# A triangular solve in pairs of heads: the second head set six rounds behind the first

## The chip, the cores and the metric

The kernel runs on one core of a Trainium2 chip. The metric is the device time of one execution in microseconds (us), the median of several runs. The engines are named as in the profile: PE (TensorE, with PEld for its weight loads), DVE (VectorE), ACT (ScalarE), POOL (GpSimd) and SP (SyncE).

## The reference

The kernel computes three layers on 512 tokens of width 1024 (two mixer layers and a third with routed experts). The change touches one step of the first layer, inside the RWKV-7 part, which has 8 heads of width 64. The core of it:

```python
A_ab = pair(a_dec, b_inv, strict)      # strictly lower triangular
A_ak = pair(a_dec, k_inv, strict)
A_rb = pair(r_dec, b_inv, incl)
A_rk = pair(r_dec, k_inv, incl)
rhs = jnp.concatenate([a_dec, jnp.einsum('bhnls,bhnsv->bhnlv', A_ak, v)], axis=-1)
sol = lax.linalg.triangular_solve(jnp.eye(L, dtype=F32) - A_ab, rhs,
                                  left_side=True, lower=True, unit_diagonal=True)
z_state, z_local = sol[..., :N], sol[..., N:]
y_local = jnp.einsum('bhnls,bhnsv->bhnlv', A_rk, v)
```

So for each head a unit lower triangular matrix is inverted by products, and the inverse is applied to two right-hand sides. The scan over chunks that follows uses z_state, z_local, A_rb and y_local.

## The kernel before

The kernel is a list of stages. In each stage every engine has a queue written out by hand, and at the end of each stage PE, ACT and DVE meet at a barrier (`meet`, L2717): each one adds to `stage_done` and waits until all three have done so. The solve, `rwkv_solve`, is one such stage; `rwkv_prepare` is before it and `rwkv_scan` after it.

The solve works on chunks of 64 tokens; a 128x128 tile holds two chunks on its diagonal, and the 512 tokens are four tiles (`TT`). All products of one kind for a head are four f32 matmuls (`mm`), which fill one PSUM bank of 128x512; the trace shows each of the four as two matmul records, so one `mm` is 8 records. A transpose is one record.

The eight heads are four pairs: `a` counts pairs (0 to 3), `q` the two heads of a pair (0 and 1). Head `q` has four of the eight banks (`4 * q` on) and seven buffers of its own (`buf[q]`: M, D, ET, AK, X, M2, D2), which all pairs use again. The heads of a pair also sit on different halves of the partitions (`r`) in the inputs and in two outputs.

A head is solved in 11 rounds, `g` = 1 to 11. In each round PE multiplies (L1516 to L1546), and then DVE, ACT or both move the results from the banks to SBUF, where the head's next round reads them:

- round 1: 4 `mm` of 64 rows (32 records); DVE makes six products with masks (L1587 to L1592)
- round 2: 4 `mm`; DVE one product (L1594), ACT three copies (L1557 to L1559)
- round 3: 4 `mm`; DVE one sum (L1596), ACT three copies (L1561 to L1563)
- round 4: 2 `mm`; DVE one sum (L1596), ACT one copy (L1565)
- round 5: 1 `mm`; DVE one sum (L1596)
- round 6: 4 transposes (L1538); ACT one copy (L1567)
- round 7: 1 `mm`; ACT one copy (L1569)
- rounds 8, 9, 10: 1 `mm` each; DVE one sum each (L1598)
- round 11: 2 `mm`; ACT two copies (L1571, L1572)

Before each round PE waits until DVE and ACT have finished what they had to do for this head's earlier rounds (`done`, waits at L1498 and L1500); DVE and ACT wait until PE has multiplied the round (`multiplied`). All three counts run over both heads: one semaphore for each engine (`pe_step`, `dve_step`, `act_step`), shared with other stages. The order in every queue is pair, then round, then head:

```python
for a in range(4):
    for g in range(1, 12):
        for q in range(2):
```

Of the kernel before, what the change touches and what calls it, by code (L numbers as in the profile page):

```python
# [24 lines left out]
ALU = mybir.AluOpType  # L25
# [3 lines left out]
P = 128  # L29
D = 1024  # L30
KB = D // P
T = 512
TT = T // P
M = 256
# [114 lines left out]
def program(nc, d, out):  # L149

    ctx = ExitStack()
    with ctx:
# [1315 lines left out]

        def rwkv_solve():
# [3 lines left out]
            p0 = pe_step.plan(4 * 22)  # L1473
            v0, a0 = dve_step.plan(4 * 2 * len(ON_DVE)), act_step.plan(4 * 2 * len(ON_ACT))
# [5 lines left out]
            def multiplied(g, a, q):  # L1480
                return p0 + 22 * a + 2 * (g - 1) + q + 1

            def done(groups, base, g, a, q):

                before = [n for n in groups if n < g]
                pair, last = (a, before[-1]) if before else (a - 1, groups[-1])
                return 0 if pair < 0 else base + 2 * len(groups) * pair + 2 * groups.index(last) + q + 1

            def pe(pe):
                for a in range(4):  # L1490
                    for g in range(1, 12):
                        for q in range(2):
                            B, r = buf[q], slice(64 * q, 64 * q + 64)
                            bank = [tiles(banks[:, 4 * q + n, :]) for n in range(4)]
                            half = [banks[:, 4 * q + n, 0:256].rearrange("p (a v) -> p a v", a=TT) for n in range(4)]
                            hc = slice((2 * a + q) * 64, (2 * a + q) * 64 + 64)
                            if n := done(ON_DVE, v0, g, a, q):
                                pe.wait_ge(dve_step.sem, n)  # L1498
                            if n := done(ON_ACT, a0, g, a, q):
                                pe.wait_ge(act_step.sem, n)  # L1500

                            def mm(out, lhs, rhs):
                                for tt in range(TT):
                                    ins = pe.matmul(out(tt), lhs(tt), rhs(tt), start=True, stop=True)
                                return ins

                            def chan(x):
                                return lambda tt: x[r, a, tt * P:(tt + 1) * P]

                            def blk(x):  # L1510
                                return lambda tt: tiles(x)[:, tt, :]

                            def to_bank(n):
                                return lambda tt: bank[n][:, tt, :]

                            if g == 1:  # L1516
                                mm(to_bank(0), chan(b_inv), chan(a_dec))
                                mm(to_bank(1), chan(a_dec), chan(b_inv))
                                mm(to_bank(2), chan(k_inv), chan(a_dec))
                                ins = mm(to_bank(3), chan(b_inv), chan(r_dec))  # L1520
                            elif g == 2:
                                mm(to_bank(0), chan(k_inv), chan(r_dec))
                                mm(lambda tt: half[1][:, tt, :], blk(B["AK"]), lambda tt: v_tok[:, tt, hc])
                                mm(to_bank(2), blk(B["M"]), blk(B["D"]))
                                ins = mm(to_bank(3), blk(B["D"]), blk(B["M"]))
                            elif g == 3:
                                mm(lambda tt: bank[0][r, tt, :], lambda tt: v_tok[:, tt, hc], blk(B["D"]))
                                mm(to_bank(1), blk(B["D2"]), blk(B["X"]))
                                mm(to_bank(2), blk(B["M2"]), blk(B["D2"]))
                                ins = mm(to_bank(3), blk(B["D2"]), blk(B["M2"]))  # L1530
                            elif g == 4:
                                mm(to_bank(1), blk(B["D"]), blk(B["X"]))
                                ins = mm(to_bank(2), blk(B["M"]), blk(B["D"]))
                            elif g == 5:
                                ins = mm(to_bank(1), blk(B["M2"]), blk(B["X"]))
                            elif g == 6:
                                for tt in range(TT):
                                    ins = pe.transpose(bank[2][:, tt, :], tiles(B["X"])[:, tt, :], mat["ident"])  # L1538
                            elif g == 7:
                                ins = mm(to_bank(3), blk(B["ET"]), blk(B["D2"]))  # L1540
                            elif g in (8, 9, 10):
                                ins = mm(to_bank(1), blk(B["D"]), blk(B[{8: "X", 9: "M", 10: "D2"}[g]]))
                            else:
                                mm(lambda tt: bank[2][r, tt, :], lambda tt: a_tok[:, tt, hc], blk(B["M"]))
                                ins = mm(lambda tt: half[3][:, tt, :], blk(B["M"]),
                                         lambda tt: B["AK"][:, tt * 64:(tt + 1) * 64])  # L1546
                            ins.then_inc(pe_step.sem, 1)

            def act(act):
                for a in range(4):  # L1550
                    for g in ON_ACT:
                        for q in range(2):
                            B, r, h = buf[q], slice(64 * q, 64 * q + 64), 2 * a + q
                            bk = [banks[:, 4 * q + n, :] for n in range(4)]
                            act.wait_ge(pe_step.sem, multiplied(g, a, q))
                            if g == 2:
                                act.copy(B["AK"][:, 0:256], bk[1][:, 0:256])  # L1557
                                act.copy(B["D2"], bk[2])
                                ins = act.copy(B["M2"], bk[3])  # L1559
                            elif g == 3:  # L1560
                                act.copy(RW["y_local"][r, a, :], bk[0][r, :])  # L1561
                                act.copy(B["D"], bk[2])
                                ins = act.copy(B["M"], bk[3])  # L1563
                            elif g == 4:
                                ins = act.copy(B["M2"], bk[2])  # L1565
                            elif g == 6:
                                ins = act.copy(B["D2"], bk[2])  # L1567
                            elif g == 7:
                                ins = act.copy(B["D"], bk[3])  # L1569
                            else:  # L1570
                                act.copy(RW["zs"][r, a, :], bk[2][r, :])  # L1571
                                ins = act.copy(RW["z_local"][:, :, q * 256 + a * 64:q * 256 + a * 64 + 64],  # L1572
                                               bk[3][:, 0:256].rearrange("p (a v) -> p a v", a=TT))
                            ins.then_inc(act_step.sem, 1)

            def dve(dve):
# [3 lines left out]
                for a in range(4):  # L1580
                    for g in ON_DVE:
                        for q in range(2):
                            B, h = buf[q], 2 * a + q
                            bk = [tiles(banks[:, 4 * q + n, :]) for n in range(4)]
                            dve.wait_ge(pe_step.sem, multiplied(g, a, q))
                            if g == 1:
                                link["dve"](dve.tensor_tensor(tiles(B["M"]), bk[0], each("s16u"), ALU.mult))  # L1587
                                dve.tensor_tensor(tiles(B["ET"]), bk[0], each("off16u"), ALU.mult)
                                dve.tensor_tensor(tiles(B["D"]), bk[1], each("s16l"), ALU.mult)
                                dve.tensor_tensor(tiles(B["AK"]), bk[2], each("s64u"), ALU.mult)  # L1590
                                dve.tensor_tensor(tiles(RW["arb"][h]), bk[3], each("i64u"), ALU.mult)
                                ins = dve.tensor_tensor(tiles(B["X"]), tiles(B["M"]), each("ident"), ALU.add)  # L1592
                            elif g == 2:
                                ins = dve.tensor_tensor(tiles(B["D"]), bk[0], each("i64u"), ALU.mult)  # L1594
                            elif g in (3, 4, 5):
                                ins = dve.tensor_tensor(tiles(B["X"]), tiles(B["X"]), bk[1], ALU.add)  # L1596
# [1318 lines left out]
```

## Time and profile before

| what | before |
|---|---|
| median of 3 runs | 3664.03 us (3662.86 to 3676.01) |
| profiled execution | 3670.56 us |
| its span, first to last instruction | 3668.7 us |
| mean granted TensorE clock | 0.922 of full speed |
| PE busy | 3292.8 us, 90% of the span |
| PEld busy | 2694.6 us, 73% |
| DVE busy | 2373.9 us, 65% |
| ACT busy | 1579.4 us, 43% |
| POOL busy | 185.8 us, 5% |

The solve lies between 310 and 493 us of the span. A line of the trace by windows gives a stretch and its length, the busy times of PE, PEld, DVE, ACT and POOL, each with its number of instructions, then PEclk (the clock that was granted to TensorE, 1.00 being 2.4 GHz and 0.50 being 1.2 GHz), the busy share of the DMA engines and GB/s. A line of the timeline gives the start, the duration of the merged group, the engine and line, the operation, what it writes and reads, and the number of instructions; in brackets how long the engine was idle before it and who released it. The matmuls of the solve carry line L1504, the transposes L1538.

### The profile page before, as it was taken

What the parts mean: (1) busy time and instruction counts of PE and PEld (TensorE: products, weight loads), DVE (VectorE), ACT (ScalarE), POOL (GpSimd) and SP (SyncE); (2) the same over time, 40 slices, a digit from 0 to 9 for tenths busy, and PEclk for the clock granted to TensorE, in tenths of its full rate; (3) what the DMA queues carried; (4) which work ended last, traced back from release to release, by engine and by line L of the source; (5) the groups of instructions that cost most, each with busy time, mean ns of one, the idle gap of its engine ahead of it and who ended that gap; (6) DMA issues with size and microseconds to landing.
All of it is one profiled execution on the core that took longest, in us unless ns stands there. A gap on an engine that the chain in (4) does not pass through costs nothing.

```text
span 3668.7 us, 42312 instructions
## 1 busy us (share of the span) xinstructions
PE 3292.8 (90%) x15690; PEld 2694.6 (73%) x15690; DVE 2373.9 (65%) x2354; ACT 1579.4 (43%) x1593; POOL 185.8 (5%) x212
## 2 busy tenths in 40 slices
PE   7867988999999847999999697768999999999996
PEld 6757977878788625877778574657888888888884
DVE  4545426467745355557763536558999999999995
ACT  2231214332223144342222213326777777777772
POOL 0000000000000000000000000000111111111110
PEclk9957978999999977999999797869999999999997
DMA  5200002334433201333433220129999999999993
GB/s 177 81 1 1 1 13 87 107 99 150 141 115 107 66 12 40 98 117 125 150 114 104 86 87 6 55 113 363 379 385 385 378 391 376 388 382 382 386 377 139
DMA packets 118821, 638.43 MB, mean 174 GB/s; under 512 B 13416, under 2 KB 13416, under 8 KB 68784
## 3 DMA queue, kind: packets, MB, share of 16 engines
q1 hardware_dynamic: 98592, 560.52, 40.9%
q0 software_dynamic: 20112, 76.24, 6.9%
q8 instruction: 86, 1.41, 0.2%
q14 instruction: 31, 0.25, 0.0%
HBM read 612.07 MB, written 24.64 MB: 174 GB/s over the span
## 4 chain that ended last, share of the span: by engine, by line
PE 72%; DVE 10%; ACT 2%; issue 1%; DMA 1%; DVEq 1%; SPq 0%; ACTq 0%; POOLq 0%
PE banks L328 24%; PE banks L2415 19%; PE banks L2432 9%; PE banks L920 7%; PE banks L341 2%; PE banks L1793 1%; DVE chunk_split L301 1%; PE banks L2409 1%; PE banks L2400 1%; PE banks L2421 1%; PE banks L578 1%; PE banks L601 1%; DVEq L2717 0%; PE banks L1162 0%; DVE scratch L1002 0%
## 5 line engine op out<-in xcount | busy, mean ns | idle before, releaser
L328 PE MATMUL banks<-x_scratch,chunk_split 128*128 128x512 f32 x3648 | 845.2, 392 | 36.7 <-DVE x_scratch L315 22.7
L328 PEld LDWEIGHTS banks<-x_scratch,chunk_split 128*128 128x128 f32 x3648 | 686.3, 189 | 189.7 <-issue 47.1
L295 ACT CAST chunk_split<-weight_ring 128x1024 fp32r<-128x1024 f32 x292 | 306.2, 1049 | 987.8 <-PE banks L328 739.2
L2415 PE MATMUL banks<-pair_split,rows 128*128 128x512 f32 x3072 | 710.0, 392 | 0.0
L2415 PEld LDWEIGHTS banks<-pair_split,rows 128*128 128x128 f32 x3072 | 578.6, 188 | 126.6
L301 DVE TENSOR_TENSOR chunk_split<-weight_ring,chunk_split 128x1024 fp32r<-128x1024 f32 x292 | 357.0, 1223 | 228.9 <-ACT chunk_split L295 220.4
L2432 PE MATMUL banks<-pair_split,hidden_t 128*128 128x512 f32 x1536 | 361.4, 394 | 6.1 <-DVE hidden_t L2527 6.1
L2432 PEld LDWEIGHTS banks<-pair_split,hidden_t 128*128 128x128 f32 x1536 | 285.3, 189 | 69.2 <-issue 6.3
L2194 DVE TENSOR_TENSOR pair_split<-mixed,pair_split 128x2048 fp32r<-128x2048 f32 x128 | 293.0, 2290 | 34.5 <-ACT pair_split L2189 34.5
L2194 DVE TENSOR_TENSOR pair_split<-scratch,pair_split 128x2048 fp32r<-128x2048 f32 x128 | 290.4, 2288 | 36.8 <-ACT pair_split L2189 36.7
L2194 DVE TENSOR_TENSOR pair_split<-weight_ring,pair_split 128x2048 fp32r<-128x2048 f32 x128 | 290.3, 2289 | 36.1 <-ACT pair_split L2189 36.1
L2189 ACT CAST pair_split<-mixed 128x2048 fp32r<-128x2048 f32 x128 | 244.9, 1914 | 65.6 <-PE banks L2415 53.3
L2189 ACT CAST pair_split<-scratch 128x2048 fp32r<-128x2048 f32 x128 | 244.2, 1908 | 60.2 <-PE banks L2415 59.6
L2189 ACT CAST pair_split<-weight_ring 128x2048 fp32r<-128x2048 f32 x128 | 241.3, 1911 | 60.1 <-PE banks L2415 52.1
L920 PE MATMUL banks<-x_down_hi,chunk_split 128*128 128x512 f32 x448 | 141.5, 395 | 0.0
L998 DVE TENSOR_TENSOR scratch<-banks,scratch 128x512 f32<-128x512 f32 x88 | 60.7, 690 | 119.5 <-PE banks L328 119.4
L2565 POOL DMA_INDIRECT token_sums<-normed,tables x32 | 86.9, 2717 | 337.6 <-ACT normed L2478 326.8
L920 PEld LDWEIGHTS banks<-x_down_hi,chunk_split 128*128 128x128 f32 x448 | 84.2, 188 | 19.7
L328 PE MATMUL banks<-x_mix,chunk_split 128*128 128x512 f32 x384 | 89.6, 395 | 5.1 <-DVE chunk_split L301 5.1
L328 PE MATMUL banks<-x_queries,chunk_split 128*128 128x512 f32 x384 | 91.8, 398 | 0.0
L328 PE MATMUL banks<-x_proj,chunk_split 128*128 128x512 f32 x384 | 90.4, 397 | 0.0
L328 PEld LDWEIGHTS banks<-x_mix,chunk_split 128*128 128x128 f32 x384 | 73.0, 191 | 21.7 <-issue 5.5
(563 smaller groups left out, 4003.9 us busy)
## 6 DMA issues: line engine op xcount, KB each, us to landing
weight_ring<-in_weights SPq DMA_DIRECT2D x292, 512.0 KB, 3.6
mixed<-in_w SPq DMA_DIRECT2D x128, 1024.0 KB, 9.0
weight_ring<-in_w SPq DMA_DIRECT2D x128, 1024.0 KB, 7.9
scratch<-in_w SPq DMA_DIRECT2D x128, 1024.0 KB, 8.7
mixed<-in_w_ada POOLq DMA_DIRECT2D x48, 512.0 KB, 3.8
token_sums<-tables POOLq DMA_DIRECT2D x1, 2560.0 KB, 21.4
residual<-in_x POOLq DMA_DIRECT2D x4, 512.0 KB, 10.3
projected<-in_mem POOLq DMA_DIRECT2D x2, 1024.0 KB, 5.2
```

The lines of the kernel that those rows point to most:

```text
L295: act.copy(chunk_split[:, 0, at:at + KB * P], flat(ring[:, n % RING])).then_inc(chunk_hi.sem, 1)
L301: dve.tensor_tensor(chunk_split[:, 1, at:at + KB * P], flat(ring[:, n % RING]), chunk_split[:, 0, at:at + KB * P], ALU.subtract).then_inc( ...
L328: mm = pe.matmul(lin.bank(j), chunk_split[:, a, at + k * P:at + (k + 1) * P], lin.split[b][k][:, 0:lin.tokens], start=(k, a, b) == (0, 0, ...
L341: mm = pe.matmul(banks[:, into[tt], :], lin.split[b][k][:, tt * P:(tt + 1) * P], chunk_split[:, a, at:at + T], start=(k, a, b) == (0, 0, 0 ...
L578: mm = pe.matmul(score_bank(h, tt), q[:, 2 * h + kk, tt * P:(tt + 1) * P], kT[:, 2 * h + kk, :], start=kk == 0, stop=kk == 1)
L920: mm = pe.matmul(banks[:, DOWN_BANKS[m], :], chunk_split[:, a, at + (k % KB) * P:at + (k % KB + 1) * P], down.split[b][k], start=(k, a, b) ...
L998: L(dve.tensor_tensor(y, bank, norm.roots, ALU.mult))
L2189: act.copy(pair_split[s][:, 0, :], raw[r]).then_inc(pair_hi, 1)
L2194: dve.tensor_tensor(pair_split[s][:, 1, :], raw[r], pair_split[s][:, 0, :], ALU.subtract).then_inc(pair_lo, 1)
L2415: mm = pe.matmul(banks[:, n, :], rows[:, a, k, :], pair_split[k % SLOTS][:, b, n * T:(n + 1) * T], start=False, stop=(k, a) == (KB - 1, 1))
L2432: mm = pe.matmul(banks[:, 4 + n, :], hid_t[:, a, k, :], pair_split[c][:, b, at:at + T], start=(k, a, b) == (0, 0, 0), stop=(k, a) == (KB - ...
L2565: pool.indirect_dma_start(sums, bass.IndirectOffsetOnAxis(row_out, 0), y_tok, None, compute_op=ALU.add)\
```

## The change

The three loops are replaced by one list of rounds, which PE, ACT and DVE all follow. Step `n` of the list holds round `n` of head 0 (counted through all four pairs, 44 rounds) and round `n - 6` of head 1, each where it exists. So head 0 begins alone with its rounds 1 to 6, then round 7 of head 0 stands beside round 1 of head 1, and so on; head 1 ends alone. When head 0 is in the rounds 1 to 6 of pair `a`, head 1 is in the rounds 6 to 11 of pair `a - 1`. Each head has its own semaphore for each of the three engines (six in all), which count from zero; nothing is planned on the shared ones. The arithmetic, its operands, the banks and the buffers are the same.

```diff
+        solve_pe, solve_dve, solve_act = ([sem(f"solve_{e}_{q}") for q in range(2)] for e in ("pe", "dve", "act"))
...
-            p0 = pe_step.plan(4 * 22)
-            v0, a0 = dve_step.plan(4 * 2 * len(ON_DVE)), act_step.plan(4 * 2 * len(ON_ACT))
+            LAST, BEHIND = 11, 6
+            rounds = [(a, g, q) for n in range(4 * LAST + BEHIND) for q in range(2) if 0 <= n - BEHIND * q < 4 * LAST
+                      for a, g in [((n - BEHIND * q) // LAST, (n - BEHIND * q) % LAST + 1)]]
...
-            def multiplied(g, a, q):
-                return p0 + 22 * a + 2 * (g - 1) + q + 1
+            def multiplied(g, a):
+                return LAST * a + g
...
-            def done(groups, base, g, a, q):
+            def done(groups, g, a):
...
-                pair, last = (a, before[-1]) if before else (a - 1, groups[-1])
-                return 0 if pair < 0 else base + 2 * len(groups) * pair + 2 * groups.index(last) + q + 1
+                return len(groups) * a + len(before)
...
-                for a in range(4):
-                    for g in range(1, 12):
-                        for q in range(2):
...
-                            if n := done(ON_DVE, v0, g, a, q):
-                                pe.wait_ge(dve_step.sem, n)
-                            if n := done(ON_ACT, a0, g, a, q):
-                                pe.wait_ge(act_step.sem, n)
...
+                for a, g, q in rounds:
...
+                    if n := done(ON_DVE, g, a):
+                        pe.wait_ge(solve_dve[q], n)
+                    if n := done(ON_ACT, g, a):
+                        pe.wait_ge(solve_act[q], n)
...
-                            ins.then_inc(pe_step.sem, 1)
+                    ins.then_inc(solve_pe[q], 1)
```

ACT and DVE are changed in the same way: one loop over `rounds`, filtered by `ON_ACT` and `ON_DVE`, waits on `solve_pe[q]` and increments of `solve_act[q]` and `solve_dve[q]`.

## Rows read from the trace of the kernel before

**Rows 1.** Busy time by window: the four pairs of the solve.
```profile
310.33:360.79 50.46, 50.05 (x344) 47.70 (x344) 17.19 (x26) 10.26 (x20) 0.00 (x0) 0.80 0.00 1
360.79:404.84 44.05, 42.98 (x345) 40.54 (x344) 17.10 (x26) 11.21 (x22) 0.00 (x0) 0.96 0.01 1
404.84:447.30 42.46, 41.39 (x345) 39.05 (x344) 17.10 (x26) 11.22 (x22) 0.00 (x0) 1.00 0.00 1
447.30:492.61 45.31, 43.09 (x345) 40.69 (x344) 17.11 (x26) 12.17 (x24) 0.00 (x0) 0.96 0.01 1
```

**Rows 2.** The same view: start of the solve, and the stage after it.
```profile
310.33:326.27 15.94, 15.94 (x80) 15.72 (x80) 6.31 (x11) 0.00 (x0) 0.00 (x0) 0.50 0.00 1
326.27:330.03 3.76, 3.76 (x18) 3.54 (x18) 1.24 (x3) 0.00 (x0) 0.00 (x0) 0.50 0.00 0
330.03:345.00 14.97, 14.91 (x125) 14.04 (x125) 3.45 (x5) 6.48 (x13) 0.00 (x0) 1.00 0.00 1
495.00:530.00 35.00, 33.87 (x566) 31.44 (x563) 10.48 (x21) 0.00 (x0) 0.00 (x0) 0.50 0.01 2
```

**Rows 3.** Timeline, third pair: head 0's round 1 to its round 2.
```profile
404.84 2.94 PE L1504 MATMUL banks<-scratch 64*128 64x128 f32 x24
...
408.71 0.69 DVE L1587 TENSOR_TENSOR scratch<-banks,tables 128x512 f32<-128x512 f32 x1 [7.18 <-PE banks L1504]
...
411.84 0.68 DVE L1592 TENSOR_TENSOR scratch<-scratch,tables 128x512 f32<-128x512 f32 x1
...
412.58 2.19 PE L1504 MATMUL banks<-projected,scratch 64*128 64x128 f32 x16 [0.67 <-DVE scratch L1592]
```

**Rows 4.** Timeline, third pair: head 0's rounds 2, 3 and 4.
```profile
416.64 0.37 ACT L1557 COPY scratch<-banks 128x256 f32<-128x256 f32 x1 [10.73 <-PE banks L1504]
...
417.39 0.60 ACT L1559 COPY scratch<-banks 128x512 f32<-128x512 f32 x1
...
420.50 1.09 PE L1504 MATMUL banks<-scratch,projected 128*64 128x128 f32 x8
...
424.50 0.58 ACT L1561 COPY projected<-banks 64x512 f32<-64x512 f32 x1 [2.54 <-PE banks L1504]
...
425.46 0.58 ACT L1563 COPY scratch<-banks 128x512 f32<-128x512 f32 x1
...
428.08 1.87 PEld L1504 LDWEIGHTS banks<-scratch 128*128 128x128 f32 x16
...
430.18 0.69 DVE L1596 TENSOR_TENSOR scratch<-scratch,banks 128x512 f32<-128x512 f32 x1 [1.10 <-PE banks L1504]
```

**Rows 5.** Timeline, third pair: head 0's rounds 6, 8, 9 and 11.
```profile
433.89 0.47 PEld L1538 LDWEIGHTS banks<-tables,scratch 128*128 128x128 f32 x4
...
434.63 0.59 ACT L1567 COPY mixed<-banks 128x512 f32<-128x512 f32 x1 [1.79 <-PE banks L1538]
...
435.33 0.97 PEld L1504 LDWEIGHTS banks<-mixed,scratch 128*128 128x128 f32 x8
...
437.23 0.97 PEld L1504 LDWEIGHTS banks<-scratch 128*128 128x128 f32 x8
...
438.43 0.69 DVE L1598 TENSOR_TENSOR scratch<-scratch,banks 128x512 f32<-128x512 f32 x1 [3.54 <-PE banks L1504]
...
439.17 0.97 PEld L1504 LDWEIGHTS banks<-scratch 128*128 128x128 f32 x8
...
443.20 2.12 PE L1504 MATMUL banks<-scratch 128*64 128x128 f32 x16
...
445.36 0.58 ACT L1571 COPY scratch<-banks 64x512 f32<-64x512 f32 x1 [7.24 <-PE banks L1504]
445.84 0.36 ACT L1572 COPY scratch<-banks 128x256 f32<-128x256 f32 x1
```

**Rows 6.** Timeline: the same 16 records of round 2 in pairs 2 and 3.
```profile
370.56 3.29 PE L1504 MATMUL banks<-scratch 128*128 128x128 f32 x16
...
414.61 2.00 PE L1504 MATMUL banks<-scratch 128*128 128x128 f32 x16
```

More of the change, by code:

```diff
@@ L1489, in pe @@
             def pe(pe):
-                for a in range(4):
-                    for g in range(1, 12):
-                        for q in range(2):
[L1493 to L1496, printed above, removed]
-                            if n := done(ON_DVE, v0, g, a, q):
-                                pe.wait_ge(dve_step.sem, n)
-                            if n := done(ON_ACT, a0, g, a, q):
-                                pe.wait_ge(act_step.sem, n)
[L1502 to L1546, printed above, removed]
-                            ins.then_inc(pe_step.sem, 1)
@@ L1549, in act @@
-            def act(act):
[L1550 to L1574, printed above, removed]
@@ new lines, in act @@
+            def act(act):
+                for a, g, q in rounds:
+                    if g in ON_ACT:
+                        B, r, h = buf[q], slice(64 * q, 64 * q + 64), 2 * a + q
+                        bk = [banks[:, 4 * q + n, :] for n in range(4)]
+                        act.wait_ge(solve_pe[q], multiplied(g, a))
+                        if g == 2:
+                            act.copy(B["AK"][:, 0:256], bk[1][:, 0:256])
+                            act.copy(B["D2"], bk[2])
+                            ins = act.copy(B["M2"], bk[3])
+                        elif g == 3:
+                            act.copy(RW["y_local"][r, a, :], bk[0][r, :])
+                            act.copy(B["D"], bk[2])
+                            ins = act.copy(B["M"], bk[3])
+                        elif g == 4:
+                            ins = act.copy(B["M2"], bk[2])
+                        elif g == 6:
+                            ins = act.copy(B["D2"], bk[2])
+                        elif g == 7:
+                            ins = act.copy(B["D"], bk[3])
+                        else:
+                            act.copy(RW["zs"][r, a, :], bk[2][r, :])
+                            ins = act.copy(RW["z_local"][:, :, q * 256 + a * 64:q * 256 + a * 64 + 64],
+                                           bk[3][:, 0:256].rearrange("p (a v) -> p a v", a=TT))
+                        ins.then_inc(solve_act[q], 1)
@@ L1578, in each @@
                     return mat[m].unsqueeze(1).to_broadcast([P, TT, P])
[L1580 to L1596, printed above, removed]
-                            else:
-                                ins = dve.tensor_tensor(tiles(B[{8: "M", 9: "D2", 10: "M"}[g]]), tiles(B["X"]), bk[1], ALU.add)
-                            ins.then_inc(dve_step.sem, 1)
@@ new lines, in dve @@
+                for a, g, q in rounds:
+                    if g in ON_DVE:
+                        B, h = buf[q], 2 * a + q
+                        bk = [tiles(banks[:, 4 * q + n, :]) for n in range(4)]
+                        dve.wait_ge(solve_pe[q], multiplied(g, a))
+                        if g == 1:
+                            link["dve"](dve.tensor_tensor(tiles(B["M"]), bk[0], each("s16u"), ALU.mult))
+                            dve.tensor_tensor(tiles(B["ET"]), bk[0], each("off16u"), ALU.mult)
+                            dve.tensor_tensor(tiles(B["D"]), bk[1], each("s16l"), ALU.mult)
+                            dve.tensor_tensor(tiles(B["AK"]), bk[2], each("s64u"), ALU.mult)
+                            dve.tensor_tensor(tiles(RW["arb"][h]), bk[3], each("i64u"), ALU.mult)
+                            ins = dve.tensor_tensor(tiles(B["X"]), tiles(B["M"]), each("ident"), ALU.add)
+                        elif g == 2:
+                            ins = dve.tensor_tensor(tiles(B["D"]), bk[0], each("i64u"), ALU.mult)
+                        elif g in (3, 4, 5):
+                            ins = dve.tensor_tensor(tiles(B["X"]), tiles(B["X"]), bk[1], ALU.add)
+                        else:
+                            ins = dve.tensor_tensor(tiles(B[{8: "M", 9: "D2", 10: "M"}[g]]), tiles(B["X"]), bk[1], ALU.add)
+                        ins.then_inc(solve_dve[q], 1)
```

45 lines of the change are left out of this document (added).

## The prediction, made before the changed kernel was run

> **What bounds the kernel now.** I read the page first (TensorE is 90% busy and carries most of the chain that ended last), then, since only one stage is touched, the busy time by window for that stage, and last the timeline of one pair of heads, instruction by instruction.
>
> The solve runs alone: from its first matmul at 310.33 us to the next stage's first instruction at 492.61 us nothing else is on TensorE, VectorE or ScalarE, and no large transfer is under way (DMA share 0.00 to 0.01). The stages on either side wait for it at a barrier, so each microsecond of the stage is one of the kernel. It takes 182.3 us: four pairs of 50.46, 44.05, 42.46 and 45.31 us [rows 1], the last with the 1.1 us by which round 11's copies outlast TensorE (below). TensorE is busy 41.39 of the 42.46 us of the third pair; VectorE 17.10, ScalarE 11.22. So the bound is TensorE, and what it loses at full clock is little: a pair has 344 matmul records, and back to back one costs 0.1125 us (8 weight loads span 0.97 us [rows 5], 16 span 1.87 [rows 4]: 0.90 for eight more), which is 38.7 us. **All waiting and start-up between rounds together is 42.5 - 38.7 = 3.8 us per pair, 15 us in the stage: the most that any reordering can give at full clock.**
>
> The rest of the stage's loss is clock. In the first pair the granted clock was 0.50 for 310.33 to 330.03 us [rows 2], although TensorE was busy all the time; the pair took 8.0 us more than the third. In pairs 2 and 4 it fell once each, behind the two rounds 1: the 16 records of round 2 took 3.29 us against 2.00 in the pair at full clock [rows 6]; those pairs lost 1.6 and 1.7 us. In all 11.3 us, so at full clock the stage would take 171.0 us.
>
> **What the change does.** No instruction of arithmetic is added or taken away. Only the order in all three queues moves: before, round g of head 0 is followed by round g of head 1; after, by round g-6. What hides one head's evacuation is the other head's matmuls, so each evacuation must be set against its new partner. First the two prices of each round, from first weight load to the same head's next possible round (the head's chain), and what TensorE spends issuing it:
>
> - Round 1: starts 404.84, VectorE begins its six products at 408.71 and ends them at 412.52, round 2 starts at 412.58: chain 7.74, of which TensorE 3.6 [rows 3].
> - Round 2: 412.58 [rows 3] to ScalarE's first copy 416.64 and last copy's end 417.99, plus 0.11 from a copy's end to the next load (434.63 + 0.59 = 435.22 to 435.33): chain 5.52, TensorE 3.9 [rows 3 to 5].
> - Round 3: 420.50 to 424.50 to 426.04, plus 0.11: chain 5.65, TensorE 3.9 [rows 4].
> - Round 4: 428.08 to 430.18, plus 0.69 and 0.05: chain 2.84, TensorE 2.0 [rows 4].
> - Rounds 5, 8, 9, 10: 437.23 to 438.43 to 439.17: chain 1.94, TensorE 1.0. Round 7, copied by ScalarE (1.20 + 0.59 + 0.11): 1.90, TensorE 1.0. Round 6, transposes, 433.89 to 434.63 to 435.33: chain 1.44, TensorE 0.5 [rows 5].
> - Round 11: 443.20 to 445.36, last copy ends 446.20, plus 0.11: 3.11 until the banks are free for the head's next round 1, TensorE 2.0 [rows 5].
>
> TensorE's prices are 32 records for round 1, half of 412.58 to 420.50 and of 420.50 to 428.08 for rounds 2 and 3, 16 records and a gap for rounds 4 and 11 (2.12 to the last result), half of 1.94 for a light one. They sum to 20.9 us a head, 41.8 a pair, near the 42.46 of [rows 1], so the prices hold the small gaps already. Before, each long evacuation lies beside an equally long block: round 1's 3.87 us beside the other head's 3.6 us of round 1, which left a wait of 0.67 us [rows 3].
>
> After, with the order 1(0) 6(1) 2(0) 7(1) 3(0) 8(1) 4(0) 9(1) 5(0) 10(1) 6(0) 11(1) 7(0) 1(1) 8(0) 2(1) 9(0) 3(1) 10(0) 4(1) 11(0) 5(1), I place each round at the later of "TensorE is done" and "the head's chain allows it". Counting from 1(0) = 0: 6(1) 3.6 to 4.1; 2(0) only at 7.74, **3.64 us idle**; 7(1) 11.64; 3(0) 13.26, 0.62 idle; 8(1) 17.16; 4(0) 18.91, 0.75 idle; 9(1) 20.91; 5(0) 21.91; 10(1) 22.91; 6(0) 23.91; 11(1) 24.85, 0.44 idle; 7(0) 26.85; 1(1) 27.96, 0.11 idle; 8(0) 31.56; 2(1) only at 35.70, **3.14 us idle**; 9(0) 39.60; 3(1) 41.22, 0.62 idle; 10(0) 45.12; 4(1) 46.87, 0.75 idle; 11(0) 48.87; 5(1) 50.87; next 1(0) 51.98, 0.11 idle. The period is 51.98 us, +9.5 on 42.46: 10.2 us of idle on 41.8 of work. VectorE's queue gives no further loss: 8(0)'s one product stands behind 1(1)'s six, but 9(0) comes only after 2(1), which waits for the same six.
>
> Start and end stand alone now. Head 0 runs rounds 1 to 6 with no partner: 7.74 + 5.52 + 5.65 + 2.84 + 1.94 + 1.44 = 25.1; round 7 takes 1.0, and from 1(1) to the next 1(0) it is 24.0: 50.15. Three periods more: 206.1. Head 1 then finishes alone: round 6 starts at 206.9, and 1.44 + 1.90 + 3 x 1.94 + 3.00 lead to 219.1. **At full clock 219.1 against 171.0: +48.1 us.**
>
> The semaphores: six of its own instead of three shared ones. The same number of waits and increments on the same instructions; I cost it at nothing (bounds 0 and, at 0.05 us from an end to a start for each of 88 rounds, 4 us either way; the nearest row is that 0.05 itself [rows 5], and it is unchanged in kind).
>
> **The clock's share.** The trace has no TensorE wait as long as 3 us inside this stage, so this is bounded from both sides. Start: round 1 at half clock costs 3.6 us more, round 2 up to 3.9 more (before, the clock came back at 330.03, 3.8 us into the 16 records that follow [rows 2]): 7.3. Of the seven later rounds 1, each is followed by half a round or a light one and then by more than 3 us of nothing. In pairs 2 and 4 less idle than that (0.67 us) brought a fall that cost 1.6; here it costs nothing where it falls into the idle itself, and 3.9 at most if the whole round 2 is slow. I take 2 each, nearest to the 1.6 of [rows 6]: 14. The end, where head 1 is alone and TensorE is under half busy: 0 to 5.9 (6.5 light blocks of 0.9), taken as 2.5. Sum 24 against 11.3 before: +12.5.
>
> Total: 48.1 + 12.5 = +61 us. The profiled execution took 3670.6 us (span 3668.7), so it would go to 3731; the median of the runs shown is 3664.0, 6.5 lower, which gives **3725 us**.
>
> On the clock the Trainium skill, page "TensorE: Matmul & The Clock Gate", section "HAM oscillation — how this bites in real kernels", states that a matmul stream with idle stretches between its bursts starts every burst at the lower clock. The trace agrees in that the clock falls behind the one stall of a pair in two pairs of three. By that rule all seven stalls cost the upper end, a rival below.
>
> **The rivals.**
>
> 1. Likeliest: stalls as placed, clock falls behind most of them. +61, from +48 to +72. Chance 0.60.
> 2. The idle is there, but the clock holds: nothing lost behind the seven stalls or at the end. 48.1 + 7.3 - 11.3 = +44: 3708. For it: in the third pair a 0.67 us wait changed nothing (1.00 throughout [rows 1]). Against: pairs 2 and 4. Chance 0.16.
> 3. Each stall is followed by a wholly slow round 2, and the end is slow: 7 x 3.9 + 5.9 + 7.3 - 11.3 + 48.1 = +77: 3741; if the slow stretch reaches into round 3 half the time, another 14: 3755. Chance 0.14.
> 4. The clock stays at 0.50 for the whole stage, as it does for 35 us in the next stage, at 97% busy [rows 2]. Work doubles to 77 us a pair, round 1's evacuation still leaves 2 x 3.2 idle: some 84 a pair, +186: 3850. Against: that stage's matmuls are 64x64, here most are whole, and the clock came back within a round 2 three times. Chance 0.04.
> 5. Other side, not slower: the skew fills the gaps of the light rounds (each 1.94 chain beside 1.9 of work now has up to 4.9) and nothing is lost in the heavy ones. That needs VectorE's 3.81 us behind round 1 to lie beside at least as much TensorE work; it decides from a partner of 3.9 us, and the new partners are 0.5 and 1.0. Its best is the 3.8 us a pair: -15, 3649; with no clock loss after the start at most 3 more, 3646. The price would only come down to it if VectorE's products ran while round 1 is still multiplying, but all six wait for the round's last matmul. Chance 0.06.
>
> **How the numbers follow.** A difference under 0.5% (18 us) can't be told from no change here. Cases 1 to 4 are all slower by more; case 5 is split at -0.5%: slower 0.94, same 0.05, faster 0.01. The range takes in cases 1, 2 and most of 3 and leaves out 4 and 5: 3703 (case 2, less 5 for the bound on semaphores) to 3752.
>
> **What would show it.** In the changed kernel's timeline: after each round 1 of either head, a TensorE idle of 3.1 to 3.7 us released by VectorE's last product (line "ident" add); waits of 0.6 to 0.8 us released by ScalarE behind rounds 2 and 3; head 0's rounds 1 recurring each 52 us (up to 56 with clock); a lead-in of 26 us (about 33 with the slow start) before head 1's first matmul; an end of some 12 us with head 1 alone; a mean clock of the stage of about 0.85 instead of 0.93. VectorE's and ScalarE's busy sums stay at 68 and 45 us. It is wrong if the period is under 45 us, if the idle behind round 1 is under 2 us, or if some other stage moves by more than a few us.

## The result

| | before | after |
|---|---|---|
| median | 3666.94 us (4 runs, 3662.86 to 3676.01) | 3730.36 us (4 runs, 3729.72 to 3734.55) |
| ratio | | 1.0172, 95% interval 1.0150 to 1.0194 |
| profiled execution | 3670.56 us | 3734.55 us |
| span | 3668.7 us | 3732.6 us |
| mean clock of the span | 0.922 | 0.918 |
| solve stage | 182.3 us | 250.4 us |
| mean clock of the stage | 0.93 | 0.85 |

The kernel became 63 us slower (3730.4 - 3666.9). The profiled executions differ by 64 us: the solve takes 68.1 more and everything else together 4.2 less. Those 4.2 are not the change's: the stages before and after it are the same, and they move by more than that from run to run (below). Of lag1 below, one execution of four took 3955.2 us at a mean clock of 0.80, and every comparison leaves it out.

The first lines of the page of after:

```profile
span 3732.6 us, 42312 instructions
...
PE 3312.4 (89%) x15690; PEld 2709.9 (73%) x15690; DVE 2373.2 (64%) x2354; ACT 1579.2 (42%) x1593; POOL 187.5 (5%) x212
```

The same 42312 instructions, DVE and ACT as busy as before; PE's 20 us more are matmuls that ran at the lower clock (in the stage PE is busy for 201.4 us instead of 177.5). Busy time by window, after: head 0 alone (start to head 1's first matmul), the rest of that first pair, three periods, head 1 alone, the stage, and one round 2.

```profile
306.47:342.43 35.96, 26.35 (x132) 24.37 (x132) 6.53 (x10) 4.07 (x8) 0.00 (x0) 0.63 0.00 0
342.43:369.63 27.20, 22.72 (x161) 21.23 (x161) 7.85 (x13) 5.02 (x10) 0.00 (x0) 0.87 0.00 1
369.63:427.69 58.06, 48.36 (x344) 45.08 (x345) 17.09 (x27) 11.10 (x22) 0.00 (x0) 0.88 0.00 1
427.69:485.75 58.06, 48.35 (x345) 45.07 (x345) 17.11 (x27) 11.10 (x22) 0.00 (x0) 0.88 0.00 1
485.75:543.80 58.05, 48.30 (x344) 44.99 (x344) 17.11 (x27) 11.10 (x22) 0.00 (x0) 0.88 0.00 1
543.80:556.84 13.04, 7.36 (x52) 6.10 (x52) 2.67 (x5) 2.13 (x4) 0.00 (x0) 1.00 0.00 1
306.47:556.84 250.37, 201.44 (x1376) 186.84 (x1376) 68.37 (x105) 44.52 (x88) 0.00 (x0) 0.85 0.00 1
...
435.40:442.33 6.93, 6.93 (x32) 6.71 (x33) 0.00 (x0) 0.00 (x0) 0.00 (x0) 0.53 0.00 0
```

The 344 records that took 42.46 us in a pair at full clock [rows 1] take 58.06 here, with the same DVE and ACT time inside. The timeline of after, from head 0's round 1 of the third pair to the end of its round 2 (against [rows 3] and [rows 6]):

```profile
427.69 2.91 PE L1504 MATMUL banks<-scratch 64*128 64x128 f32 x24
...
431.43 0.66 PE L1538 MATMUL banks<-tables,projected 128*128 128x128 f32 x4
431.54 0.69 DVE L1585 TENSOR_TENSOR scratch<-banks,tables 128x512 f32<-128x512 f32 x1 [3.20 <-PE banks L1504]
...
434.66 0.68 DVE L1590 TENSOR_TENSOR scratch<-scratch,tables 128x512 f32<-128x512 f32 x1
...
435.40 3.97 PE L1504 MATMUL banks<-projected,scratch 64*128 64x128 f32 x16 [3.31 <-DVE scratch L1590]
...
439.16 3.34 PE L1504 MATMUL banks<-scratch 128*128 128x128 f32 x16
...
442.54 0.37 ACT L1556 COPY scratch<-banks 128x256 f32<-128x256 f32 x1 [9.83 <-PE banks L1504]
```

Round 1 to round 2 is 435.40 - 427.69 = 7.71 us, as before (7.74). Beside it lie only the four transposes of head 1's round 6, so PE is idle for 3.31 us until DVE's last product has ended. And then the 32 records of round 2 take 6.93 us at a clock of 0.53, where at full clock they took 3.9. The other six rounds 2 behind a stall of this kind, of either head, show the same: 6.9 us at 0.53 or 0.54. Who PE waited for, over the whole stage of after (engine and line, released by: us in total, times, longest):

```profile
PE banks L1504 <- DVE scratch L1590: 13.9, 4, 4.0
PE banks L1504 <- DVE projected L1590: 11.2, 4, 2.8
PE banks L1504 <- DVEq L2715: 7.1, 1, 7.1
PE banks L1504 <- ACT scratch L1562: 4.2, 4, 1.7
PE banks L1504 <- ACT mixed L1562: 3.8, 4, 1.0
PE banks L1504 <- ACT scratch L1558: 3.5, 4, 1.6
PE banks L1504 <- ACT projected L1558: 2.6, 4, 0.6
```

L1590 is DVE's last product of round 1, L1558 and L1562 are ACT's last copies of rounds 2 and 3; the third line lies ahead of the stage. 25.1 us behind the eight rounds 1, where before there was one wait of 0.67 us in a pair [rows 3]; 14.1 behind rounds 2 and 3.

### The profile page after: what moved, and what is told of

Its sections match the earlier page's. It is cut to its first block, busy times and chain, and to the rows that moved or that the text cites. A ratio compares the mean times of both kernels' runs of the same rounds, so it can differ in the third digit from the quotient of the medians.

```text
span 3732.6 us, 42312 instructions
## 1 busy us (share of the span) xinstructions
PE 3312.4 (89%) x15690; PEld 2709.9 (73%) x15690; DVE 2373.2 (64%) x2354; ACT 1579.2 (42%) x1593; POOL 187.5 (5%) x212
## 4 chain that ended last, share of the span: by engine, by line
PE 71%; DVE 10%; ACT 2%; issue 1%; DMA 1%; DVEq 0%; SPq 0%; ACTq 0%; POOLq 0%
PE banks L328 24%; PE banks L2413 19%; PE banks L2430 9%; PE banks L920 7%; PE banks L341 2%; PE banks L1791 1%; DVE chunk_split L301 1%; PE banks L2407 1%; PE banks L2398 1%; PE banks L2419 1%; PE banks L578 1%; PE banks L601 1%; DVEq L2715 0%; PE banks L1162 0%; DVE scratch L1002 0%
```

## The experiments

Two theories stood against each other at first. A: the loss comes from which round stands beside which, through idle behind round 1, and the clock adds to it. B: it comes from something else that the change brings, its semaphores, the lag as such, or the stretches where a head runs alone. "Lag" is the constant `BEHIND`; all kernels here are the changed kernel with the edits shown. Where a comparison is with the changed kernel, its 3730.4 us and its stage of 250.4 us are meant.

### The order of before with the semaphores of the change (lag0)

```diff
-            LAST, BEHIND = 11, 6
+            LAST, BEHIND = 11, 0
```

> The changed kernel with a lag of 0 rounds instead of 6: the order of before, the six semaphores of the change. Theory (the partner of a round makes the loss, the semaphores nothing): the time of before within 4 us, the third pair again 42.5 us long, one wait of about 0.7 us behind each round 1. Rival (semaphores of one's own cost or gain): 88 rounds at 0.05 us, some 4 us slower or faster, and a period other than 42.5.

Measured: 3668.18 us (10 runs) against 3670.43 of before, ratio 1.000 (0.9984 to 1.0016). Windows of one pair, then of the stage:

```profile
402.29:444.75 42.46, 41.39 (x345) 39.05 (x345) 17.08 (x26) 11.21 (x22) 0.00 (x0) 1.00 0.00 1
307.88:494.83 186.95, 182.18 (x1376) 172.43 (x1376) 68.43 (x104) 44.83 (x88) 0.00 (x0) 0.90 0.00 1
```

The third pair takes 42.46 us, to the hundredth what it was. The stage as a whole took 4.7 us more than before (186.95 against 182.3), but not through the semaphores: the first three pairs differ from those of before by 0.1 us at most, and the fourth took 50.08 us at a clock of 0.86, where in before it took 45.31 at 0.96. PE's idle in the stage is the same to the hundredth, 4.77 us. So the semaphores cost nothing, and one and the same order can lose some 5 us more or less by the clock.

### A lag of one round (lag1), and of eleven (lag11)

```diff
-            LAST, BEHIND = 11, 6
+            LAST, BEHIND = 11, 1
```

> Lag of 1 round. Theory: placing the rounds by their prices gives a period of 45.8 us against 42.8 for lag 0 (2.1 us of idle behind head 0's round 1, whose partner is now round 11, and 0.2 to 0.8 in four other places), 187 against 172 us for the stage at full clock: +15, and 5 to 8 more if the clock falls behind the 2.1 us of idle in each pair: +15 to +23 on before, 3682 to 3690. Rival (only the stretches where one head runs alone cost): the lone stretches are one round at each end, +3 to +5.

Measured: 3693.72 us (3 runs) against 3670.43, ratio 1.0063 (1.0038 to 1.0088), +23 by the medians, the upper end of what was expected. The stage took 201.4 us, +19.1 on before; its two middle periods, and the longest entry of what PE waited for:

```profile
364.68:413.41 48.73, 45.27 (x344) 42.30 (x345) 17.19 (x27) 11.07 (x22) 0.00 (x0) 0.93 0.00 1
413.41:460.56 47.15, 43.69 (x345) 40.73 (x345) 17.18 (x27) 11.07 (x22) 0.00 (x0) 0.96 0.00 1
...
PE banks L1504 <- DVE scratch L1590: 9.5, 4, 4.0
```

Placing gave 45.8; the rest is clock (0.93 and 0.96). One round of lag already costs about a third of what six cost, though the heads run alone for one round only: not what the rival of this run says.

```diff
-            LAST, BEHIND = 11, 6
+            LAST, BEHIND = 11, 11
```

> Lag of 11 rounds: each round again beside the same round of the other head, but of the pair before. Theory (partner): in the middle a period of 42.8 us and waits of under 1 us as before; only the lone stretches cost, 11 rounds at either end, 36 us of chain each for 21 us of work: stage 201 against 172 at full clock, +29, and 2 to 6 more for the clock at the start and behind the one long idle at the end: +31 to +35 on before, 3695 to 3702, some 30 us faster than lag 6. Rival (the lag itself costs, each round of it about 10 us): slower than lag 6, 3780 or more.

Measured: 3711.69 us against 3670.43, ratio 1.012 (1.0097 to 1.0144), +41; more than the 31 to 35 expected, but far from the 3780 of the rival and 19 us faster than lag 6. Windows: head 0 alone, three pairs, head 1 alone.

```profile
308.11:352.50 44.39, 30.64 (x172) 27.77 (x173) 8.59 (x13) 5.50 (x11) 0.00 (x0) 0.74 0.00 0
352.50:396.56 44.06, 42.99 (x345) 40.63 (x345) 17.09 (x26) 10.26 (x20) 0.00 (x0) 0.96 0.00 1
396.56:440.61 44.05, 42.98 (x346) 40.53 (x345) 17.09 (x26) 11.21 (x22) 0.00 (x0) 0.96 0.01 1
440.61:484.28 43.67, 41.45 (x346) 39.09 (x345) 17.09 (x26) 12.16 (x24) 0.00 (x0) 1.00 0.00 1
484.28:526.49 42.21, 28.35 (x172) 25.60 (x172) 8.59 (x13) 5.71 (x11) 0.00 (x0) 0.80 0.00 1
```

With the same round beside it again, a pair takes 44 us as it did before the change [rows 1], although the lag is longer than ever. What is left is the two lone stretches, 86.6 us for one pair's work. The stage is 218.4 us, +36.1 on before and +31.4 on lag 0's; +31 to +35 on before was expected. So the lag by itself costs nothing, and of theory B only the lone stretches are left. That the profiled execution, 3695.9 us, lies inside what was expected is luck: its scan, the stage behind the solve, took 27.1 us where before's took 39.9 (below). With before's scan it would have been 3708.7 us, an estimate from these two. It is the lowest of four at a mean clock of 0.925; the others, 3709.0 to 3719.6, have 0.916 to 0.918, which fits the longer scan for 12.8 us of their 13 to 24. The rest is open.

### The idle filled with dummy matmuls (fill6)

```diff
+                    if g == 2 and (a, q) != (0, 0):
+                        for tt in range(14):
+                            pe.matmul(tiles(banks[:, 4 * (1 - q), :])[:, tt % TT, :], mat["ident"], mat["ident"],
+                                      start=True, stop=True)
                     if n := done(ON_DVE, g, a):
```

> Lag 6, and TensorE gets 14 dummy f32 matmuls of 128x128 (the unit matrix by itself, 3.15 us at full clock) ahead of each round 2 but the very first, into a bank that nobody needs then: the idle behind round 1 is filled, nothing else is changed. Theory (the idle makes the clock fall, and this costs 3.0 us behind each of seven rounds 1): clock 1.00 through each round 2, period 52.0 to 52.5 us instead of 58.1, 18 to 21 us faster than lag 6. Rival (it is round 1's own matmuls, of 64 rows, that bring the clock down): the clock still falls, and with 14 matmuls at half clock ahead of it each round 2 comes up to 2.5 us later: equal or up to 15 us slower than lag 6.

Measured: 3710.80 us, 19.6 less than the changed kernel (ratio to before 1.0105, 1.0080 to 1.0130, against 1.0172). A period by window, and in it the dummies (L1499) and the round 2 behind them:

```profile
370.47:422.70 52.23, 48.46 (x401) 45.50 (x401) 17.10 (x27) 11.10 (x22) 0.00 (x0) 1.00 0.00 1
...
374.70 3.29 PE L1499 MATMUL banks<-tables 128*128 128x128 f32 x28
378.18 2.19 PE L1508 MATMUL banks<-projected,scratch 64*128 64x128 f32 x16 [0.18 <-DVE scratch L1594]
380.20 2.00 PE L1508 MATMUL banks<-scratch 128*128 128x128 f32 x16
```

98 more matmuls make the kernel 20 us faster. The median could mislead here, with two executions at 3705 us and two at 3717, but the stage shows the gain by itself: 230.25 us against 250.37, 20.1 less. Nothing else was touched: round 2 starts 7.7 us after round 1 as before, but at full clock. This takes the loss apart: 52.23 a period is the waiting alone (51.98 had been worked out), and 58.06 - 52.23 = 5.8 us a period is the clock, 2.9 for each round 1. It also shows that round 1's own matmuls of 64 rows don't bring the clock down by themselves: they are the same here, and it stayed at 1.00. Whether they help the idle to do it was not tested. The waits hint that they do: 0.67 us behind them came with the fall in pairs 2 and 4 of before, while 0.64 to 0.95 us behind rounds 2 and 3 of the changed kernel never did.

### Shorter evacuation of round 1 (xlate6, drop2)

xlate6 signals round 1 ahead of the product X, which round 2 does not read. drop2 leaves out two of the six products instead.

```diff
-                            dve.tensor_tensor(tiles(RW["arb"][h]), bk[3], each("i64u"), ALU.mult)
-                            ins = dve.tensor_tensor(tiles(B["X"]), tiles(B["M"]), each("ident"), ALU.add)
+                            dve.tensor_tensor(tiles(RW["arb"][h]), bk[3], each("i64u"), ALU.mult)\
+                               .then_inc(solve_dve[q], 1)
+                            dve.tensor_tensor(tiles(B["X"]), tiles(B["M"]), each("ident"), ALU.add)
...
-                        ins.then_inc(solve_dve[q], 1)
+                        if g > 1:
+                            ins.then_inc(solve_dve[q], 1)
```

> Lag 6; VectorE signals the end of round 1 after its fifth product, and the sixth (X, which no one reads before round 3) runs behind the signal. Theory (the idle behind round 1 ends when VectorE's products end): each of the eight idles is 0.60 us shorter (2.7 instead of 3.3 by the matmul rows for head 0, 2.2 instead of 2.8 for head 1), clock as before: period 56.9 instead of 58.1, some 5 us faster than lag 6, 3725. Rival (something else releases round 2): no change.

> Lag 6, and two of VectorE's six products of round 1 are left out (the masks of ET and of arb), so part of the computation is missing. Theory: the chain of round 1 is 1.2 us shorter in each of eight heads, -9.6 us at an unchanged clock; each 1.2 us less idle may also keep the clock up behind some of the seven, up to 3.0 us each: 10 to 20 us faster than lag 6, 3710 to 3720. Rival (VectorE is not what the idle waits for, or the clock is what counts alone): under 3 us.

Measured: xlate6 3722.96 us, 7.4 less than the changed kernel; drop2 3717.40, 13.0 less. Periods of xlate6 (three), one wait of it, and periods of drop2 (two):

```profile
364.99:422.06 57.07, 48.70 (x344) 45.41 (x345) 17.09 (x27) 11.10 (x22) 0.00 (x0) 0.88 0.00 1
422.06:477.06 55.00, 47.12 (x345) 44.07 (x345) 17.11 (x27) 11.20 (x22) 0.00 (x0) 0.91 0.00 1
477.06:532.00 54.94, 46.92 (x344) 43.89 (x344) 17.05 (x26) 11.01 (x22) 0.00 (x0) 0.91 0.00 1
```
```profile
429.17 3.04 PE L1504 MATMUL banks<-projected,scratch 64*128 64x128 f32 x16 [2.71 <-DVE scratch L1589]
```
```profile
366.10:420.16 54.06, 47.13 (x345) 43.95 (x345) 14.72 (x23) 11.10 (x22) 0.00 (x0) 0.91 0.00 1
420.16:473.34 53.18, 46.51 (x345) 43.26 (x345) 14.71 (x23) 11.20 (x22) 0.00 (x0) 0.90 0.00 1
```

The wait of 3.31 became 2.71, the 0.60 of one product, and the releaser is now the fifth product (2.12 in drop2): DVE is what the idle waits for. The shorter idle alone gives 1.2 us a period in xlate6 and 2.4 in drop2; measured were 1.0 to 3.1 and 4.0 to 4.9. What is over goes with a clock that falls a little less (up to 0.91 for 0.88). The stages took 237.5 and 231.7 us, 12.9 and 18.7 less than the changed kernel's, of which 4.8 and 9.6 are the shorter idle of eight rounds 1; in xlate6 6.1 of the 12.9 lie ahead of the first of the periods shown. xlate6 was expected to gain 5 us in all, its clock as before: that part was wrong.

### The same on the order of before, and a warm start (xlate0, warm0)

xlate0 is xlate6 with lag 0. warm0 adds, in the stage before, ahead of TensorE's last transposes:

```diff
+                    else:
+                        for i in range(20):
+                            pe.matmul(banks[:, 4 + i % 4, 0:P], mat["ident"], mat["ident"], start=True, stop=True)
                     transposes(pe, 0 + 4 * n, end if n == 0 else RW["k_end_t"]).then_inc(pe_step.sem, 1)
```

> Lag 0 (the order of before) with the same early signal after VectorE's fifth product. Theory: the 0.67 us wait behind head 0's round 1 shrinks to 0.1, 2.4 us for four pairs; if the clock then no longer falls in two of the pairs, 3.3 more: 2 to 6 us faster than before, 3661 to 3665. Rival: the wait moves to head 1's round 2, whose products stand behind in VectorE's queue: 0 to 1 us.

> As the last, and in the stage before, where TensorE waits for VectorE from 303.4 to 310.3 us, 20 dummy f32 matmuls stand ahead of its last 16 transposes (about 6 us of work instead of idle). Theory (the first pair takes 8 us more than the third only because it begins at half clock and the rounds 1 keep the clock that they find): the clock is at 1.00 when the solve begins and stays, first pair 42.5 instead of 50.5: 8 us faster than the last, 3654 to 3657. Rival (the 64-row matmuls at the start bring the clock down by themselves): clock at 0.50 again after the first rounds, 0 to 3 us gained.

Measured: xlate0 3666.69 us (12 runs) against 3667.84, ratio 0.9989 (0.9975 to 1.0003); warm0 3664.98, ratio 0.9984 (0.9971 to 0.9996). The first three pairs of xlate0, then warm0's first pair, the solve's first 3.5 us and the 13 behind them:

```profile
305.89:356.22 50.33, 49.92 (x344) 47.68 (x344) 17.17 (x26) 10.26 (x20) 0.00 (x0) 0.81 0.00 1
356.22:398.08 41.86, 41.39 (x345) 39.05 (x344) 17.00 (x26) 11.21 (x22) 0.00 (x0) 1.00 0.00 1
398.08:439.94 41.86, 41.39 (x345) 39.05 (x345) 17.00 (x26) 11.21 (x22) 0.00 (x0) 1.00 0.00 1
```
```profile
306.21:353.84 47.63, 47.22 (x345) 44.98 (x345) 17.18 (x26) 10.25 (x20) 0.00 (x0) 0.86 0.00 1
...
306.21:309.70 3.49, 3.49 (x26) 3.49 (x27) 0.00 (x0) 0.00 (x0) 0.00 (x0) 0.83 0.00 0
309.70:323.00 13.30, 13.30 (x72) 13.03 (x71) 7.55 (x12) 0.00 (x0) 0.00 (x0) 0.53 0.00 0
```

In the stage xlate0 did what was expected: the wait of 0.67 us [rows 3] is gone, a pair takes 41.86 instead of 42.46, and the clock fell in none of the pairs 2 to 4; the stage is 177.1 us against 182.3. The same holds in the other four kernels with this order and signal (warm0, scan2, scan4, scan1): a period of 41.85 or 41.86 us in each, where before and lag0, with the wait, both had the fall in pairs 2 and 4. The profiled executions of before and xlate0 differ by 4.6 us (3670.56 and 3665.96). The median doesn't show it: the expected time was missed. warm0's first pair is 2.7 us shorter, not 8: the clock was up when the solve began, fell within the first round and stayed down until the first whole round 2, which is what the rival said.

Where the 5 us of xlate0 went is seen in the stage behind, the scan, whose code is the same in all these kernels. Its window in before and in lag0:

```profile
492.61:532.52 39.91, 37.94 (x640) 35.16 (x640) 12.18 (x25) 0.00 (x0) 0.00 (x0) 0.52 0.01 2
```
```profile
494.83:521.97 27.14, 22.34 (x640) 20.38 (x640) 12.18 (x25) 0.00 (x0) 0.00 (x0) 1.00 0.01 3
```

The same 640 matmul records, 39.9 us at half clock or 27.1 at full clock, a difference of 12.8 us that no edit made: the profiles of lag0, lag11 and drop2 have the short scan, those of before, after and the others so far the long one. In the long one the clock is still up when the scan begins and falls in its first 2 us (0.52 over the whole). The difference is more than twice what xlate0 had to gain, so a median that mixes the two can hide it. Directly it is known of the profiled executions only, but the mean clocks of the others fit such a mix: of the 23 executions of before that xlate0 stands against, nine have 0.924 to 0.926 (3662.7 to 3667.0 us) and fourteen 0.919 to 0.922 (3667.4 to 3681.0); of xlate0's twelve, eleven have 0.921 to 0.923 and one 0.930, at 3649.3 us.

### The scan kept at full clock (scan2, scan4, scan1)

On top of xlate0, dummy matmuls ahead of the scan's two waits in each chunk, n = 2, 4 and 1, and 6 before the first (36, 66 and 21 in all):

```diff
+                def extra(n):
+                    for i in range(n):
+                        pe.matmul(banks[:, 7, 0:P], mat["ident"], mat["ident"], start=True, stop=True)
...
+                    extra(2 if c else 6)
                     pe.wait_ge(dve_step.sem, v0 + 2 * c + 1)
...
+                    extra(2)
                     pe.wait_ge(dve_step.sem, v0 + 2 * c + 2)
```

> As xlate0 (lag 0, early signal), and in the scan stage behind the solve TensorE gets dummy f32 matmuls of 128x128 into a bank that nobody uses: 6 at the start, and 2 ahead of each of its two waits in each of the 8 chunks. In the profiles so far the scan took 39.9 us at a clock of 0.52 in most executions and 27.1 us at 0.92 in two of them, with its 64x64 matmuls and gaps of 0.3 to 0.9 us. Theory (it keeps the clock that it finds, and falls only at random at its start): the whole-array matmuls in the gaps keep the clock at 1.00 in every execution: scan 27 to 29 us, 8 to 12 us faster than xlate0's median, 3655 to 3659. Rival (64x64 matmuls bring the clock down whatever stands in the gaps): scan at 40 us plus 3 to 7 for the dummies at half clock, 3668 to 3674.

> The same with 4 instead of 2 dummy matmuls ahead of each wait of the scan (0.9 us at full clock, longer than some of the gaps). Theory: the clock holds at least as surely as with 2, the dummies stick out of the gaps by up to 0.4 us in 16 places: scan 30 to 35 us, 3658 to 3665. Rival: half clock all the same and 14 us of dummies more, 3675 to 3682.

> As scan2 with one dummy matmul ahead of each wait of the scan instead of two. In scan2 the scan took 32.6 us, 3.95 a chunk, against 3.35 a chunk where the clock was up without dummies and 5.0 where it was down. Theory: the second dummy of each pair sticks out of its gap; with one the chunk takes 3.4 to 3.6 us at full clock, scan 28 to 30 us, 3 to 4 us faster than scan2: 3657 to 3660. Rival (one is too little to hold the clock): chunks of 5 us in most executions, 3666 or more.

Measured: scan2 3661.50 us (12 runs), ratio 0.9973 (0.9959 to 0.9986); scan4 3665.05, ratio 0.9987 (0.9975 to 1.0000); scan1 3651.97 (6 runs) against 3672.35, ratio 0.9952 (0.9935 to 0.9969). The scan's window in scan2, scan4 and scan1:

```profile
483.42:516.04 32.62, 32.51 (x712) 29.43 (x712) 12.17 (x25) 0.00 (x0) 0.00 (x0) 1.00 0.01 3
```
```profile
483.23:522.54 39.31, 39.20 (x772) 36.12 (x772) 12.18 (x25) 0.00 (x0) 0.00 (x0) 1.00 0.01 3
```
```profile
483.56:513.21 29.65, 29.55 (x682) 26.07 (x682) 12.17 (x25) 0.00 (x0) 0.00 (x0) 1.00 0.01 3
```

The clock is at 1.00 in all three, and the other executions agree: scan2's twelve have a mean clock of 0.926 to 0.929, where eleven of xlate0's twelve have 0.921 to 0.923. scan4's dummies cost all that the clock gave; the expected 30 to 35 us and scan2's 27 to 29 were too low by 4 at least. The gaps are shorter than those expectations took them to be: in lag0's scan, behind the 1.57 us at its start, PE's idle by the matmul records is 0.15 to 0.42 us, not 0.3 to 0.9. So the second dummy of a gap costs 0.20 us (15 more take the scan from 29.65 to 32.62) and the third and fourth 0.22 each (30 more, to 39.31), nearly or wholly the 0.225 us that one takes. (The 0.92 in scan2's expectation is the mean over 40 us; over the short scan alone it is 1.00.) With one it takes 29.7 us. This version beats both kernels: the order of before, the earlier signal and the steady scan are together worth 0.5%. It has fewer runs than scan2, and of its 20 us on the medians some 15 are accounted for (5 in the solve, 10 in the scan).

## Why the prediction was right

The forecast was 3725 us, from 3703 to 3752; the result 3730. The mechanism came out as forecast, and two sizes did not. By its own steps:

- **What bounds the stage, and that it stands alone: right.** The stage's loss is the kernel's (68 and 64 us in the profiled executions).
- **The prices and the placing: right.** The worked-out period was 51.98 us, fill6's at full clock 52.23. The idle behind round 1 was to be 3.64 and 3.14, released by the last product: 3.31 and 2.81 between the matmuls' records, 3.55 and 3.00 between the weight loads'. Head 1's lie a little under the 3.1 named as a sign. Rounds 2 and 3 were to leave 0.62 and 0.75: 0.64 and 0.83 to 0.95.
- **The semaphores at nothing: right**, by lag0.
- **The end: right.** Worked out 13.0 us (206.1 to 219.1) and a clock cost of 0 to 5.9, taken as 2.5; it took 13.04, at 1.00.
- **The clock: right in kind, too small behind the stalls.** I took 2 us for each of seven; all seven fell, and it was 2.9 to 3.0 each (58.06 - 51.98 over two; 6.93 against 3.9 for one round 2). I leaned on the 1.6 us of [rows 6], whose idle was a fifth as long. The term that was mis-sized is this one, by 7 us in all: the period was 58.06 us, over the "up to 56 with clock" that was named as a sign.
- **The start: too small.** 35.96 us to head 1's first matmul instead of 26.1 at full clock, 9.8 more where 7.3 was taken: the slow stretch reached through round 2 into round 3.
- Together the clock cost 31 us in the stage, not 24, against 11.3 before. With +48.1 that is +68 for the stage, as measured. The kernel's +64 lies nearer to the forecast of +61 because the rest was 4.2 us shorter in the profiled run, and that is luck, as it is that the end (2.5 us less than the sum held) makes up for the start (2.5 more).

The Trainium skill, page "TensorE: Matmul & The Clock Gate", section "HAM oscillation — how this bites in real kernels", says of a stream of bursts with long waits between them that each burst starts at the lower clock. The trace agrees for the seven stalls of 2.8 to 3.3 us: each round 2 behind them had 0.53 or 0.54. It does not show it for the waits of 0.64 to 0.95 us behind rounds 2 and 3, where the clock stayed at 1.00. Of the rivals, case 1's range (+48 to +72) holds the result. Case 2 (the clock holds) fell with the 0.53 of the rounds 2; case 3 wanted each round 2 wholly slow and a slow end: the rounds 2 came near it (3.0 of 3.9 us), the end was at 1.00. No pair stayed at half clock throughout (case 4, whose +186 is also not what its own 84 us a period gives: four of them and 2 x 11.2 us for the lone stretches are 358 us, +176 on 182.3). The other side (case 5) failed where it was said to: DVE's 3.81 us found a partner of 0.5 and 1.0 us.

## What to carry to other kernels

Two chains that take turns on one engine hide each other's evacuations only if long evacuations stand beside long blocks: before shifting them, write down for each round both prices, the chain and what the engine issues, and place them in the new order by hand; it gave the period to 0.5% here. Idle of TensorE costs more than its length when the clock falls behind it: here 3.3 us of idle cost 3 more, while 0.64 to 0.95 us behind rounds 2 and 3 cost only themselves. And look at the granted clock of the stages that were not edited before reading a gain of some microseconds from a median.

## What was not expected of the hardware

- 98 useless matmuls made a kernel 20 us faster (fill6, 20.1 in its stage), and 21 in the scan made it 10 us shorter (scan1), only by the clock: 1.00 where it was 0.88 and 0.52.
- One and the same stage (the scan, 640 records of 64x64 and, at full clock, gaps of 0.15 to 0.42 us) ran at 0.52 for 39.9 us or at 1.00 for 27.1 us, with no edit to it. Where it took 39.9 us the clock fell in the first 2 us and didn't come back. What decides whether it falls was not settled; whole-array matmuls in the gaps kept it up in the three profiles taken with them.
- The clock that was up at the start of the solve fell within 3.5 us of matmuls of 64 rows (warm0), behind 16 transposes of 1.9 us in all and 2.6 us of idle, while in fill6 and xlate0 it stayed up through the same matmuls with no such idle around them.
